# RWKV-7 chunk loop: each step for all four pairs of heads at once, and the state in two buffers by turns

## What is computed

```
S_t = S_{t-1} diag(decay_t) - (S_{t-1} kk_t) b_t^T + v_t k_t^T ;  y_t = S_t r_t
def step(S, inp):
    r_t, w_t, k_t, v_t, kk_t, b_t = inp
    sa = jnp.einsum('bhij,bhj->bhi', S, kk_t)
    S = S * w_t[:, :, None, :] - sa[..., None] * b_t[:, :, None, :] + v_t[..., None] * k_t[:, :, None, :]
    y = jnp.einsum('bhij,bhj->bhi', S, r_t)
```

## Time and profile before

| | before |
|---|---|
| median of 3 runs | 4177.87 us (4173.76 to 4178.23) |
| the profiled execution: its own time, its span | 4186.01 us, 4184.1 us |
| busy: TensorE (PE), its weight loads, VectorE (DVE), ScalarE (ACT) | 90%, 68%, 54%, 17% |
| mean granted TensorE clock | 0.94 of full speed |

### The profile page before, as it was taken

The page is one execution under the profiler, slowest core; times in us unless marked ns, Lnnn a source line. Parts: engine busy times, 40 slices in busy tenths (PEclk is TensorE's granted clock), DMA queues, the critical chain, the costliest instruction groups (busy, mean ns, idle before and its releaser), DMA issues.

```text
span 4184.1 us, 69508 instructions
## 1 busy us (share of the span) xinstructions
PE 3777.9 (90%) x29136; PEld 2862.2 (68%) x29136; DVE 2257.8 (54%) x4486; ACT 727.6 (17%) x1520; POOL 555.0 (13%) x444
## 2 busy tenths in 40 slices
PE   7999686999979999999889996769999799999995
PEld 4566454887547888888655664548865488888884
DVE  2599875666245243434636987566662442434345
ACT  1311363332010000000112114523320100000000
POOL 0041100000011122212100410000000112212220
PEclk9999797999789999999999997969997899999997
DMA  2001100000110111112210110100001111111121
GB/s 110 26 31 37 40 18 6 3 3 26 56 66 31 47 45 41 41 42 90 76 40 22 34 40 11 39 1 3 3 25 61 61 41 41 41 41 51 41 82 51
DMA packets 43376, 163.62 MB, mean 39 GB/s; under 512 B 5056, under 2 KB 5072, under 8 KB 42720
## 3 DMA queue, kind: packets, MB, share of 16 engines
q1 hardware_dynamic: 27648, 100.68, 7.0%
q0 software_dynamic: 15456, 58.85, 3.8%
HBM read 135.07 MB, written 23.49 MB: 38 GB/s over the span
## 4 chain that ended last, share of the span: by engine, by line
PE 80%; DVE 14%; issue 3%; ACT 2%; POOL 1%; DMA 0%; DVEq 0%; ACTq 0%; POOLq 0%
PE ps L701 37%; PE ps L650 17%; PE ps L731 7%; PE ps L618 5%; PE ps L880 1%; PE ps L892 1%; DVE arena L1394 1%; PE ps L934 1%; DVE arena L1515 1%; PE ps L905 1%; PE ps L662 1%; PE ps L628 1%; DVE arena L1291 1%; DVE arena L1517 1%; PE ps L994 1%
## 5 line engine op out<-in xcount | busy, mean ns | idle before, releaser
L701 PE MATMUL ps<-arena 128*128 128x261 f32 x4096 | 924.7, 383 | 5.7 <-POOL arena L537 2.9
L701 PEld LDWEIGHTS ps<-arena 128*128 128x128 f32 x4096 | 775.1, 189 | 135.1 <-issue 5.4
L701 PE MATMUL ps<-arena,ring 128*128 128x261 f32 x3072 | 705.2, 385 | 22.3 <-DVE arena L1747 22.0
L650 PE MATMUL ps<-arena,ring 128*128 128x348 f32 x2304 | 700.7, 463 | 23.3 <-DVE arena L1270 18.9
L701 PEld LDWEIGHTS ps<-arena,ring 128*128 128x128 f32 x3072 | 584.3, 190 | 123.0 <-issue 21.1
L650 PEld LDWEIGHTS ps<-arena,ring 128*128 128x128 f32 x2304 | 438.1, 192 | 284.8 <-issue 56.8
L731 PE MATMUL ps<-arena 64*64 64x64 f32 (+1 forms) x13600 | 513.0, 226 | 97.7 <-DVE arena L1469 43.2
L731 PEld LDWEIGHTS ps<-arena 64*64 64x64 f32 x13600 | 467.7, 135 | 141.9 <-DVE arena L1515 48.8
L1394 DVE TENSOR_SCALAR_CACHE_REDUCE arena<-arena,little 128x384 uint8<-128x384 f32 (+6 forms) x448 | 416.9, 990 | 3.1
L1336 DVE TENSOR_TENSOR arena<-aux,ps 128x522 f32<-128x522 f32 x160 | 111.8, 699 | 422.8 <-PE ps L701 422.2
L537 POOL TENSOR_TENSOR arena<-ring 128x512 f32<-128x512 f32 x128 | 169.1, 1321 | 1107.2 <-DMA ring<-units 1101.8
(11 more groups left out here) (223 smaller groups left out, 3571.6 us busy)
## 6 DMA issues: line engine op xcount, KB each, us to landing
ring<-units SPq DMA_DIRECT2D x192, 512.0 KB, 3.7
h_scratch<-arena POOLq DMA_DIRECT2D x24, 522.0 KB, 3.1
arena<-h_scratch POOLq DMA_DIRECT2D x24, 522.0 KB, 8.3
arena<-h_in POOLq DMA_DIRECT2D x16, 522.0 KB, 10.0
out<-arena POOLq DMA_DIRECT2D x8, 522.0 KB, 3.1
arena<-att_scratch POOLq DMA_DIRECT2D x2, 2080.0 KB, 9.0
att_scratch<-arena POOLq DMA_DIRECT2D x16, 256.0 KB, 2.9
aux<-rope POOLq DMA_DIRECT2D x2, 1044.0 KB, 12.5
```

The costliest lines, as they stand in the source:

```text
L650: ins = mm(ps[:, b + s, 0:SW], ring[:, r * D + k * P:r * D + (k + 1) * P], tile(U0, k)[:, slice_(s)], start=(k == 0), stop=(k == KT - 1))
L701: ins = mm(acc_at(n)[:, s], lhs[:, k * P:(k + 1) * P], rhs(k)[:, s * HALF:(s + 1) * HALF], start=(k == 0), stop=(k == KT // 2 - 1))
```

## The change

Everything in the chunk loop that was done per half is done once for all four pairs: 256 columns in one ScalarE copy or one VectorE instruction, one semaphore count in place of two, one PSUM bank in place of two. The X product goes to bank 0, MX to bank 4, XMT to bank 7, W to bank 0, U to bank 2, the change of the state to bank 4. The state has two buffers `s0` and `s1`: `new_state` reads the one of the finished chunk and writes the other, and it stands in one piece behind the vector instructions of the inverse's start. The matmuls of the state's change for all pairs stand ahead of those of the output `y`, with a semaphore count behind each of the two groups; before, both were issued pair by pair. The arithmetic is the same.

```
@@ pe_chunk
                 for n in range(1, LEVELS):
-                    for half in range(2):
-                        pe.wait_ge(S["m_ready"], w.next("m_ready"))
-                        for g in pairs(half):
-                            ins = heads(half_bank(0, 1, g), off[:, g], m[:, g])
-                        ins.then_inc(S["x_ready"], 1)
+                    pe.wait_ge(S["m_ready"], w.next("m_ready"))
+                    for g in range(4):
+                        ins = heads(col(0, g), off[:, g], m[:, g])
+                    ins.then_inc(S["x_ready"], 1)
                     if n == 1:
-                        pe.wait_ge(S["s_out"], w.next("s_out", 2))
-                    for half in range(2):
-                        pe.wait_ge(S["x_out"], w.next("x_out"))
-                        pe.wait_ge(S["mt_ready"], w.next("mt_ready"))
-                        if n < LEVELS - 1:
-                            for g in pairs(half):
-                                ins = heads(half_bank(4, 7, g), mt[:, g], x[:, g])
-                            ins.then_inc(S["mx_ready"], 1)
-                        for g in pairs(half):
-                            ins = heads(half_bank(2, 5, g), x[:, g], mt[:, g])
+                        pe.wait_ge(S["s_out"], w.next("s_out"))
+                    pe.wait_ge(S["x_out"], w.next("x_out"))
+                    pe.wait_ge(S["mt_ready"], w.next("mt_ready"))
+                    if n < LEVELS - 1:
+                        for g in range(4):
+                            ins = heads(col(4, g), mt[:, g], x[:, g])
                         ins.then_inc(S["mx_ready"], 1)
+                    for g in range(4):
+                        ins = heads(col(7, g), x[:, g], mt[:, g])
+                    ins.then_inc(S["mx_ready"], 1)
...
-                for half in range(2):
-                    pe.wait_ge(S["u_out"], w.next("u_out"))
-                    for g in pairs(half):
-                        heads(half_bank(4, 7, g), km[:, g], vm[:, g], start=True, stop=False)
-                        heads(half_bank(4, 7, g), bm[:, g], u_[:, g], start=False, stop=True)
-                        y = col(3, g)
...
-                    ins.then_inc(S["s_ready"], 1)
+                pe.wait_ge(S["u_out"], w.next("u_out"))
+                for g in range(4):
+                    heads(col(4, g), km[:, g], vm[:, g], start=True, stop=False)
+                    ins = heads(col(4, g), bm[:, g], u_[:, g], start=False, stop=True)
+                ins.then_inc(S["s_ready"], 1)
+                for g in range(4):
+                    heads(col(3, g), s_[:, g], rt[:, g], start=True, stop=False)
...
@@ act_chunk
-                    for half in range(2):
-                        act.wait_ge(S["x_ready"], w.next("x_ready"))
-                        go(cb("x", 256)[:, P * half:P * (half + 1)], ps[:, half, 0:P],
-                           ACT.Copy).then_inc(S["x_out"], 1)
+                    act.wait_ge(S["x_ready"], w.next("x_ready"))
+                    go(cb("x", 256), ps[:, 0, 0:256], ACT.Copy).then_inc(S["x_out"], 1)
@@ new_state
-                s_ = cb4("s")[:, 2 * half:2 * half + 2]
+                s_, new = cb4("s%d" % odd), cb4("s%d" % (1 - odd))
                 dve.wait_ge(S["s_ready"], w.next("s_ready"))
-                do(v.tensor_tensor(s_, s_, bank4(7 if half else 4, CH)[:, 0:2], ALU.add))
+                do(v.tensor_tensor(new, s_, bank4(4, CH), ALU.add))
@@ dve_chunk
-                    for half in range(2):
-                        m, mt, off, abt = (half2(k, half) for k in ("m", "mt", "off", "abt"))
-                        if n < LEVELS - 1:
-                            dve.wait_ge(S["mx_ready"], w.next("mx_ready"))
-                            v.tensor_tensor(off, abt, level[n], ALU.mult)
-                            v.tensor_tensor(m, m, bank2(4, 7, half), ALU.subtract).then_inc(S["m_ready"], 1)
+                    if n < LEVELS - 1:
                         dve.wait_ge(S["mx_ready"], w.next("mx_ready"))
-                        v.tensor_tensor(mt, mt, bank2(2, 5, half), ALU.subtract).then_inc(S["mt_ready"], 1)
+                        v.tensor_tensor(off, abt, level[n], ALU.mult)
+                        v.tensor_tensor(m, m, bank4(4, CH), ALU.subtract).then_inc(S["m_ready"], 1)
+                    dve.wait_ge(S["mx_ready"], w.next("mx_ready"))
+                    v.tensor_tensor(mt, mt, bank4(7, CH), ALU.subtract).then_inc(S["mt_ready"], 1)
```

More of the change, by code:

```diff
@@ L774, in pe_chunk @@
[L774 to L789 removed]
+                for g in range(4):
+                    heads(col(0, g), kap[:, g], s_[:, g], start=True, stop=False)
+                    ins = heads(col(0, g), akt[:, g], vm[:, g], start=False, stop=True)
@@ new lines, in pe_chunk @@
+                ins.then_inc(S["w_ready"], 1)
+                pe.wait_ge(S["mt_ready"], w.next("mt_ready"))
+                pe.wait_ge(S["w_out"], w.next("w_out"))
+                for g in range(4):
+                    ins = heads(col(2, g), mt[:, g], x[:, g])
+                ins.then_inc(S["u_mm"], 1)
+                pe.wait_ge(S["u_out"], w.next("u_out"))
+                for g in range(4):
+                    heads(col(4, g), km[:, g], vm[:, g], start=True, stop=False)
+                    ins = heads(col(4, g), bm[:, g], u_[:, g], start=False, stop=True)
@@ L791, in pe_chunks @@
+                ins.then_inc(S["s_ready"], 1)
+                for g in range(4):
+                    heads(col(3, g), s_[:, g], rt[:, g], start=True, stop=False)
+                    heads(col(3, g), vm[:, g], lk[:, g], start=False, stop=False)
+                    ins = heads(col(3, g), u_[:, g], lb[:, g], start=False, stop=True)
+                ins.then_inc(S["s_ready"], 1)
             def pe_chunks(w):
@@ L1099, in act_chunk @@
                 for n in range(1, LEVELS):
-                    for half in range(2):
-                        act.wait_ge(S["x_ready"], w.next("x_ready"))
-                        go(cb("x", 256)[:, P * half:P * (half + 1)], ps[:, half, 0:P],
-                           ACT.Copy).then_inc(S["x_out"], 1)
+                    act.wait_ge(S["x_ready"], w.next("x_ready"))
+                    go(cb("x", 256), ps[:, 0, 0:256], ACT.Copy).then_inc(S["x_out"], 1)
                     if n == 1:
-                        act.wait_ge(S["s_out"], w.next("s_out", 2))
+                        act.wait_ge(S["s_out"], w.next("s_out"))
                         if not last:
                             act_factors(w, i + 1, 1 - odd)
[L1109 to L1113, removed]
+                for ready, dst, b, done in (("w_ready", "x", 0, "w_out"), ("u_mm", "u", 2, "u_out")):
+                    act.wait_ge(S[ready], w.next(ready))
+                    go(cb(dst, 256), ps[:, b, 0:256], ACT.Copy).then_inc(S[done], 1)
                 act.wait_ge(S["s_ready"], w.next("s_ready", 2))
@@ L1225, in _ @@
                 act_factors(w, 0, 0)
-                with w.loop(NCH // 2, s_out=4, turned_ready=2, x_ready=4 * (LEVELS - 1), w_ready=4, u_mm=4,
+                with w.loop(NCH // 2, s_out=2, turned_ready=2, x_ready=2 * (LEVELS - 1), w_ready=2, u_mm=2,
                             s_ready=4) as i:
@@ L1482, in new_state @@
                 dve.wait_ge(S["s_out"], w.next("s_out"))
+                w.skip("s_ready", 1)
             def dve_chunk(w, i, odd, first=False, last=False):
-                half2 = lambda name, half: cb4(name)[:, 2 * half:2 * half + 2]
-                bank2 = lambda b0, b1, half: bank4(b1 if half else b0, CH)[:, 0:2]
-                level = [over2(const("levels")[:, j * CH:(j + 1) * CH]) for j in range(LEVELS - 1)]
+                level = [over4(const("levels")[:, j * CH:(j + 1) * CH]) for j in range(LEVELS - 1)]
@@ new lines, in dve_chunk @@
+                m, mt, off, abt = (cb4(n) for n in ("m", "mt", "off", "abt"))
+                dve.wait_ge(S["gram_ready"], w.next("gram_ready"))
+                v.tensor_tensor(abt, bank4(6, P)[:, :, 0:CH], over4(const("strict")), ALU.mult).then_inc(S["dve_done"], 1)
+                abt_done = w.next("dve_done")
+                v.tensor_tensor(m, bank4(1, CH), over4(const("inv0")), ALU.mult).then_inc(S["dve_done"], 1)
+                m_done = w.next("dve_done")
+                dve.wait_ge(S["dve_done"], abt_done)
```

68 lines of the change are left out of this document (22 added, 46 removed).

## The result

The changed kernel takes 4287.7 us as the median of 4 runs (4283.69 to 4289.85), against 4175.8 us (4173.55 to 4178.23) for the kernel before in the same series: a ratio of 1.0267, with a 95% interval of 1.0249 to 1.0285. The change costs 112 us; 4293 us were predicted. The profiled execution has a span of 4288.1 us and its own time of 4289.85 us.

A forecast was written before the change was run, and what follows sets the result against it. Each level, a closed round of a half through three engines, was taken to bound the loop; 3.38 us more per chunk over 34 chunks gives 115 us, 4301 on the profiled execution, 4293 on the median, range 4262 to 4340.

The forecast's parts named there:

- half 1's round: Kernel before, one level: half 1's closed round through TensorE, ScalarE and VectorE fills the whole 1.88 us period.
- The level's price: One level of the inverse in one piece: the round takes 2.70 us instead of 1.88, 0.82 more.
- The chunk's start: From the chunk's first mask product to the first MX: 3.14 us instead of 3.26, 0.12 less per chunk.
- the later arm: Before the first MX: X and its ScalarE copy end at 3.13 us, behind the state's arm at 3.09.
- The state's wait: First MX's wait for the state's second half: all but gone, bringing just 0.12 us per chunk.
- The chunk's end: XMT, W, U and state records in one piece: state's records at 17.26 us, next mark at 21.19 instead of 17.81.
- The sum: Whole kernel: 34 chunks x 3.38 us = 115 us more, 4301 on the profiled execution, 4293 on the median.
- The clock stayed at 1.00: Main case, chance 0.75: 4270 to 4315; the rival, clock falling in the levels, 4317 to 4580, chance 0.16.
- the row with a low cover at full clock: Between 560 and 565 us TensorE, covered 1.88 of 5 us, kept 1.00; taken as sign for the loop's clock.
- the records bound the level: Rival: levels stay at 1.88 us and vector waits vanish, 4106, or 4155 for the state's part only; chance 0.05.
- The cover in the loop: Sign to look for: TensorE's matmul cover in the changed chunk loop near 80%.

The follow-up runs named there:

- the kernel with the state first: Changed kernel with the new state computed before the wait for the Gram products instead of behind the mask products: 4286.5 us.
- the early mask product: Mask product computed two levels ahead in two buffers: 4248.5 us on the changed kernel, 4152.4 us on the kernel before, in halves.

## Why the prediction was right

- **What bounds the loop.** That half 1's round, and not TensorE's 91% cover, sets the level of before: shown, from both sides. The mask product taken out of it makes the kernel faster in halves (by 24 us, 18 of them in the loops) and in one piece (by 39 us), without a record fewer on TensorE. The two limits were close, though: 0.14 us per level.
- **The level's price.** 2.70 us predicted, 2.71 measured; the copy 0.38 (0.383), the vector instruction 0.42 (0.414), the burst to VectorE 0.74 (0.73), the burst to ScalarE 0.72 (0.73).
- **The chunk's start.** First MX at 3.14 predicted (the later arm's own sum gives 3.13), 3.19 measured, and ScalarE's arm the later one: shown by the kernel with the state first. The vector instructions there were miscounted ahead of the prediction: the trace of before has fifteen (one of 256 columns, fourteen of 128), not thirteen, against eight; the sum used only the eight. The state's wait was worth 0.12 on paper for this change and nothing more could be had from it in one piece; in halves it gives 14 us.
- **The chunk's end.** XMT at 13.94 (14.03 measured), W's copy at 15.60 (15.69), U's at 16.83 (16.94), the state's records at 17.26 (17.37), the next mark at 21.19 (21.31). The steps of 1.66, 0.38 and 0.85 came out as 1.66, 0.38 and 0.87.
- **The sum.** 3.38 us per chunk were predicted and 3.49 measured, 115 and 119 us; 0.1 of it is spread over the steps above. Outside the loop some 7 us of the median came back, which was not foreseen, and the two errors partly cancel: 4293 predicted, 4287.7 measured. That 115 us predicted come so near the 112 of the medians is in part luck; on the profiled execution's own time, 4301 predicted against 4289.85, the part outside the loop weighs more.
- **The rivals.** The clock stayed at 1.00 from 722 to 1078 us and from 2860 to 3214 us, all but the first microseconds of both loops, though the weight loads pause 0.5 to 0.6 us twice per level; the row with a low cover at full clock was the better guide. The Trainium skill's page "TensorE: Matmul & The Clock Gate", section "A second HAM failure mode: psum-queue depth-cycling", tells of a bf16 kernel with 512 columns per matmul whose grant swung with micro-idles between groups of matmuls; this float32 loop of 64x64 tiles does not behave so. That the records bound the level is refuted by the early mask product, in one piece outright and in halves for the kernel before. The cover in the loop was put near 80% and is 76%.

## What to carry to other kernels

When a loop is a chain of short dependent steps through several engines, add up one round of it, station by station, before merging its instructions: if the sum is the period, the parallel half is what fills the other engines' waits, and merging lengthens every station. Here fewer and larger instructions went to VectorE and ScalarE, which had idle time, and gained nothing. A station that can be computed ahead (here the mask product) was worth its full length per round in one piece, 0.34 us, but in halves 0.135 of 0.20, until TensorE's records were the limit. When a wait is removed, look for the arm that ends next, by the end times and not by the name in the brackets.

## What the runs showed of the hardware

- Half the columns save less than half the time on each station: a VectorE instruction starts 0.20 us behind the one before it with 128 columns and 0.34 with 256, a ScalarE copy takes 0.28 and 0.38, and 8 records reach ScalarE in 0.50 us where 16 take 0.73 (850.65 to 851.38 above). In halves the whole still wins, since the two rounds overlap.
- Each matmul of the code is two records in every trace here (the 8 matmuls of a product are x16). All operands are float32, so no run shows whether the type is the reason.
- How long the clock is lowered behind the loop isn't set by the instructions there alone: the same ones had a grant of 0.50 for 54.6 us in the kernel before and for 40.9 us with a pause ahead of the loop, and took 75.5 and 70.2 us. Spans of one kernel range over 17 us (4166.9 to 4184.1), and the mean clock was 0.944 at the one end and 0.940 at the other.
